# One more seven-product step in every first down pair of an MLP, with its rounding placed a group earlier

## The chip, the cores and the metric

The kernel runs on one core of one Trainium2 chip. The metric is the time of one execution in microseconds (us). Each kernel is measured in several runs, and the median counts. The traces come from one profiled execution per kernel.

## What is computed

The reference is one decoder block on 256 tokens with 2048 channels: attention and a state-space branch, merged by gates, and then an MLP. The change lies in the MLP alone:

```python
h = h + (g_attn * y_attn + g_ssm * y_ssm) @ w_out[layer]
u = rms_norm(h, mlp_norm_w[layer]) @ w_up[layer]          # 2048 -> 8192
h = h + jnp.square(jax.nn.relu(u)) @ w_down[layer]        # 8192 -> 2048
```

All is float32. The kernel splits each operand into a rounded high part and a remainder (`hi`, `lo`, both fp32r) and makes every product of three matmuls: hi by hi, lo by hi, hi by lo.

## The kernel before

**Pairs and groups.** The MLP is worked off in 16 *pairs* `m` (two column blocks of 512 each), in four rounds `q = m // 4` of one quarter of the 8192 channels. In a round `m % 4` is 0 or 1 for the two up pairs and 2 or 3 for the two down pairs. Each pair has 8 *groups* `j`. A group takes one 128 x 2048 load of weights (`raw4`, three buffers), which ScalarE rounds into `whi4` and VectorE turns into the remainder `wlo4` (two buffers each). A group (m, j) is written (2,5) below, where the first number is `m % 4`.

**Classical and seven.** A classical group makes 8 products of 128x128 by 128x512, that is 24 matmuls. A *seven* makes the same result by the Strassen-Winograd scheme with 7 products, 21 matmuls (`seven_products`, from L1134 on). It needs more from the other engines. VectorE makes sums of the weight tiles (`t_sums`, L2434 to L2439), ScalarE rounds them (`t_round`, L1723 and L1725), and VectorE makes the remainders `t_lo_` (L2424), which take the place of `t_sum`. For down pairs, four sums of activation tiles are made in each case (`f_sums`, L2505 to L2510), rounded (`f_sums_hi`, L1785), and their remainders made (`f_sums_lo`, L2514). A pair with sevens has four more PSUM banks, which are added up after the last seven of the pair (`p1_copy`, L1733, and `u_sums`, L2444 to L2449), and into `h` by `h_from_sums`. `seven(m)` gives the groups that are sevens. In the first down pair that is group 0 alone, in the second down pair 0, 3 and 5. Three forms of activation sums per round (for 0, 3, 5) are made anyway, since the second down pair uses them all.

**The order of work.** Every engine has its work in an order written out by hand, by (m % 4, j). At step j the engines prepare group j + 1: `mlp_hi` rounds its weights (L1712, or L1716 and L1718 for a seven), `mlp_lo` makes remainders (L2413, or L2418 for a seven). A seven with no seven in the two groups before it is `early`: its sums are made two groups ahead and rounded behind the weights of the group before it. `mlp_hi` waits until TensorE has let go of the buffer (`unit_used`), which for a seven means the whole group two before it.

**From an up pair to its down pairs.** At steps 0 to 5 of the next pair ScalarE works off the result of the up pair before: `relu` (L1740), `square` (L1755), `r_halve` (L1765, which splits float32 into halves of 16 bits for the transposing DMA), and, when SyncE's `r_turn` (L564) has brought the transposed halves, `f_hi` (L1777, L1781: joins the halves into `f_st`, then rounds them into `fT_hi`). VectorE follows with `f_lo` (L2521, `fT_lo`) and `f_sums`. `f_st` is one buffer: the second `f_hi` waits until `f_sums` has read the first. At (2,3) `f_hi` and `f_lo` stand before the weights of the next group (`JOIN_FIRST`), else behind them.

**Waits of TensorE.** At the head of a seven in a down pair TensorE waits for `sums_lo` of its form and for `fT_lo`. The first product of a pair that goes to banks 0 and 1 waits for `c_free`, which VectorE counts up when `h_from_banks` (L2467) has added the pair before into `h`. In a pair with a seven at group 0 that product is the one that begins with the 13th matmul.

**SyncE's queue.** It issues the loads of group j and, behind the loads of group 4 and of group 5, two transposes each (`TURN_AT`). It waits in order: for `lo_ready` of the group three before a load, and for `r_halve` before an `r_turn`.

Of the kernel before, what the change touches and what calls it, by code (L numbers as in the profile page):

```python
# [65 lines left out]
DOWN_SEVEN = (0, 3, 5)  # L66
DOWN_SEVEN_FIRST = (0,)
UP_ORDER = (0, 1, 2, 3, 4, 5, 6, 7)
# [31 lines left out]
H_SUMS = 1 if UP_SEVEN else 0  # L100
SUMS_AT = (6, 5, 5, 6)
SUMS_LATE = ((1, 6), (2, 3))
JOIN_FIRST = (2, 3)
MADE_FIRST = ()
FORMS_MADE = ((1, 4), (2, 1), (2, 3))
FORMS_HI = ((1, 5), (2, 4), (2, 5))
FORMS_LO = ((1, 6), (2, 5), (2, 6))
JOIN_AT = {1: (3, 5), 2: (3, 4)}
# [19 lines left out]
def build(nc, x, mix_norm_w, w_in, q_norm_w, k_norm_w, conv_w, conv_b, dt_bias, a_log, d_skip, ssm_norm_w,  # L128
# [13 lines left out]
    with ctx:  # L142
# [336 lines left out]
        def fp(ap):  # L479

            return ap.bitcast(f32)
# [35 lines left out]
        def _(sp):  # L517
# [213 lines left out]

            TURN_AT = (4, 5)
            for m in range(PAIRS):
# [485 lines left out]
        def _(act):  # L1219
# [577 lines left out]
            for m in range(PAIRS):  # L1797
# [3 lines left out]
                for j in range(QUADS):  # L1801
# [7 lines left out]
                    elif (m or j) and nxt[0] < PAIRS:  # L1809
                        if before is not None and (m % 4, j) == JOIN_FIRST:  # L1810
                            f_hi(before, JOIN_AT[m % 4].index(j))
                        mlp_hi(*nxt)
                        roundings(*nxt)
                    if before is not None:
# [4 lines left out]
                        if j == 1:  # L1819
                            r_halve(before, 0)  # L1820
                            square(before, 1)
# [4 lines left out]
                    for i, at_ in enumerate(FORMS_HI):  # L1826
                        if (m % 4, j) == at_:
                            f_sums_hi(m // 4, i)
# [11 lines left out]
        def _(dve):  # L1840
# [558 lines left out]

            def mlp_lo(m, j, only=None):  # L2400
                seven_, what = quads(m)[j]
# [14 lines left out]
                for i, part in enumerate((slice(1, 3), slice(3, 4))):  # L2416
                    dve.wait_ge(hi_ready, n + i + 1)
                    V.tensor_tensor(lo[:, part, :], src[:, part, :], fp(hi[:, part, :]), ALU.subtract).then_inc(lo_ready, 1)  # L2418
                for i in range(2):
                    part = slice(2 * i, 2 * i + 2)  # L2420
# [133 lines left out]
            for m in range(PAIRS):  # L2554
                k = m % 4
# [3 lines left out]
                for j in range(QUADS):  # L2559
# [6 lines left out]
                    elif j and nxt[0] < PAIRS:  # L2566
# [4 lines left out]
                        if is_seven(*nxt) and not early(*nxt):  # L2571
                            t_sums(*nxt)
                        mlp_lo(*nxt)
                    if early(*follow(m, j, 2)) and (k, j) in SUMS_LATE:
# [5 lines left out]
                    for i, at_ in enumerate(FORMS_LO):  # L2580
                        if (k, j) == at_:
                            f_sums_lo(m // 4, i)
# [187 lines left out]
```

## Time and profile before

| | us |
|---|---|
| median of 3 runs (lowest, highest) | 1977.62 (1977.33, 1977.79) |
| the profiled execution | 1977.46 |
| its span | 1975.4 |
| TensorE busy | 1968.7 |
| VectorE busy | 1488.0 |
| ScalarE busy | 1241.9 |

The span runs from the first to the last instruction; the execution's own time holds 2.1 us more. The profile's page gives the busy time of each engine. A matmul is shown with 0.39 us, but matmuls overlap, so what one costs is read from the distance of their starts. The same holds for VectorE and ScalarE, where an instruction may start about 0.1 us before the one before it ends. The timeline gives start, duration, engine, line and operands, with the idle time ahead in square brackets.

### The profile page before, as it was taken

To read this page: it belongs to the slowest core of one execution; us is meant where nothing else is said; L and a number is where in the kernel's file an instruction comes from. 1 tells how busy PE (TensorE), PEld (TensorE's weight loads), DVE (VectorE), ACT (ScalarE), POOL (GpSimd) and SP (SyncE) were. 2 spreads that over 40 slices of the span, in tenths; PEclk is the share of its full clock that TensorE was granted. 3 is DMA by queue.
4 is the path that set the end of the run, shared out by engine and by line. 5 is a ranking of instruction groups with operands and counts; after the bars stand their busy time and mean duration, and the time that the engine had idled before them with its cause. 6 is when DMAs were issued, how large, how long until landed. Compare 5 with 4: busy or idle time off the path is not lost.

```text
span 1975.4 us, 25599 instructions
## 1 busy us (share of the span) xinstructions
PE 1968.7 (100%) x9007; PEld 1629.1 (82%) x9007; DVE 1488.0 (75%) x1769; ACT 1241.9 (63%) x1427; POOL 175.1 (9%) x179
## 2 busy tenths in 40 slices
PE   9999999999999999999999999999999999999999
PEld 8888888888887888888888888888888888888887
DVE  5777777767788767676665556577898799888878
ACT  6666666767776555655674444557757855865773
POOL 2110020112232111111000000000000000000000
PEclk9999999999999999999999999999999999999999
DMA  7787887789987666665895776777666866676765
GB/s 250 207 205 201 213 205 210 213 222 247 235 228 229 197 194 200 199 194 182 218 246 190 213 214 229 213 213 217 221 201 202 245 196 208 215 224 202 229 198 171
DMA packets 332193, 419.52 MB, mean 212 GB/s; under 512 B 147248, under 2 KB 147696, under 8 KB 331840
## 3 DMA queue, kind: packets, MB, share of 16 engines
q1 hardware_dynamic: 331184, 415.23, 72.4%
q10 hardware_dynamic: 448, 2.24, 0.3%
q8 instruction: 59, 0.97, 0.2%
q0 software_dynamic: 464, 0.77, 0.2%
q14 instruction: 38, 0.31, 0.1%
HBM read 382.46 MB, written 2.16 MB: 195 GB/s over the span
## 4 chain that ended last, share of the span: by engine, by line
PE 98%; DVE 1%; ACT 1%; issue 0%; DVEq 0%; ACTq 0%
PE ps L807 20%; PE ps L809 20%; PE ps L808 20%; PE ps L1104 11%; PE ps L1109 11%; PE ps L1105 11%; PE ps L986 1%; PE ps L755 1%; PE ps L973 0%; DVE wlo L2413 0%; PE ps L819 0%; PE ps L858 0%; PE ps L881 0%; PE ps L1007 0%; ACT whi L1229 0%
## 5 line engine op out<-in xcount | busy, mean ns | idle before, releaser
L1848 DVE TENSOR_TENSOR wlo<-raw,whi 128x1024 fp32r<-128x1024 f32 x450 | 569.4, 1272 | 328.5 <-ACT whi L1229 327.0
L1229 ACT ACTIVATE whi<-raw 128x1024 fp32r<-128x1024 f32 x450 | 473.2, 1057 | 323.3 <-PE ps L809 313.1
L807 PE MATMUL ps<-whi,xT_hi 128*128 128x512 f32 x1268 | 498.3, 393 | 0.0
L809 PE MATMUL ps<-whi,xT_lo 128*128 128x512 f32 x1268 | 493.8, 389 | 0.0
L808 PE MATMUL ps<-wlo,xT_hi 128*128 128x512 f32 x1268 | 493.5, 389 | 0.0
L809 PEld LDWEIGHTS ps<-whi,xT_lo 128*128 128x128 f32 x1268 | 238.0, 188 | 50.2
L807 PEld LDWEIGHTS ps<-whi,xT_hi 128*128 128x128 f32 x1268 | 238.1, 188 | 48.9 <-issue 1.4
L808 PEld LDWEIGHTS ps<-wlo,xT_hi 128*128 128x128 f32 x1268 | 238.2, 188 | 47.3
L1712 ACT ACTIVATE whi<-raw 128x1024 fp32r<-128x1024 f32 x187 | 192.8, 1054 | 102.5 <-PE ps L1109 98.3
L2413 DVE TENSOR_TENSOR wlo<-raw,whi 128x1024 fp32r<-128x1024 f32 x186 | 219.7, 1220 | 41.4 <-ACT whi L1712 41.1
L1104 PE MATMUL ps<-whi,fT_hi 128*128 128x512 f32 x416 | 162.0, 389 | 0.2 <-DVE h L2467 0.2
L1105 PE MATMUL ps<-whi,fT_lo 128*128 128x512 f32 x416 | 161.8, 389 | 0.0
L1104 PE MATMUL ps<-whi,hT_hi 128*128 128x512 f32 x410 | 159.6, 389 | 0.0
L1105 PE MATMUL ps<-whi,hT_lo 128*128 128x512 f32 x410 | 159.5, 389 | 0.0
L1109 PE MATMUL ps<-wlo,fT_hi 128*128 128x512 f32 x416 | 114.0, 389 | 0.0
L1109 PE MATMUL ps<-wlo,hT_hi 128*128 128x512 f32 x410 | 112.1, 389 | 0.0
L807 PE MATMUL ps<-whi,sT_hi 128*128 128x512 f32 x256 | 99.6, 389 | 0.0
L808 PE MATMUL ps<-wlo,sT_hi 128*128 128x512 f32 x256 | 99.6, 389 | 0.0
L809 PE MATMUL ps<-whi,sT_lo 128*128 128x512 f32 x256 | 99.6, 389 | 0.0
L1104 PEld LDWEIGHTS ps<-whi,fT_hi 128*128 128x128 f32 x416 | 78.1, 188 | 17.0 <-ACT whi L1712 0.6
L1109 PEld LDWEIGHTS ps<-wlo,fT_hi 128*128 128x128 f32 x416 | 78.1, 188 | 16.2
L1105 PEld LDWEIGHTS ps<-whi,fT_lo 128*128 128x128 f32 x416 | 78.1, 188 | 16.2
(358 smaller groups left out, 2874.3 us busy)
## 6 DMA issues: line engine op xcount, KB each, us to landing
raw<-in_w_in SPq DMA_DIRECT2D x319, 512.0 KB, 4.3
raw<-in_w_up SPq DMA_DIRECT2D x128, 512.0 KB, 4.3
raw<-in_w_down SPq DMA_DIRECT2D x128, 512.0 KB, 4.7
raw<-in_w_ssm_out SPq DMA_DIRECT2D x64, 512.0 KB, 4.2
raw<-in_w_attn_out SPq DMA_DIRECT2D x32, 512.0 KB, 3.7
raw<-in_w_out SPq DMA_DIRECT2D x32, 512.0 KB, 4.3
arow<-arows SPq DMA_DIRECT2D x16, 512.0 KB, 4.9
x_in<-in_x SPq DMA_DIRECT2D x4, 512.0 KB, 7.8
```

The lines of the kernel that those rows point to most:

```text
L755: return nc.tensor.transpose(dst, src, ident[:, :])
L807: mm(dst, xh, whi[sl][:, kk, :], start=(s == 0 and kk == 0), stop=False)
L808: mm(dst, xh, wlo[sl][:, kk, :], start=False, stop=False)
L809: last = mm(dst, xl, whi[sl][:, kk, :], start=False, stop=(s == US - 1 and kk == UK - 1))
L986: last = mm(ps[6][d0:d0 + SHD, hh // 2 * P:(hh // 2 + 1) * P], xf[:, hh, :], M[:, hh, :], start=True, stop=True)
L1104: mm(ps[bank], xh, wh, start=first, stop=False)
L1105: mm(ps[bank], xl, wh, start=False, stop=False)
L1109: return mm(ps[bank], xh, wl, start=False, stop=(left[bank] == 0))
L1229: A(whi[s % SLOTS][:, :, :], raw[s % SLOTS][:, :, :], ACT.Copy).then_inc(hi_ready, 1)
L1712: A(dst[:, 2 * i:2 * i + 2, :], src[:, 2 * i:2 * i + 2, :], ACT.Copy).then_inc(hi_ready, 1)
L1848: V.tensor_tensor(wlo[s % SLOTS][:, :, :], raw[s % SLOTS][:, :, :], fp(whi[s % SLOTS][:, :, :]), ALU.subtract).then_inc(lo_ready, 1)
L2413: V.tensor_tensor(lo[:, part, :], src[:, part, :], fp(hi[:, part, :]), ALU.subtract).then_inc(lo_ready, 1)
```

## The change

`DOWN_SEVEN_FIRST` gets group 5 beside group 0, so that the four first down pairs (m = 2, 6, 10, 14) have two sevens in place of one. 33 sevens become 37. With it:

- ScalarE rounds the own weights of (2,5) and its sums behind the weights of (2,4), at step 3, and then the activation form for group 5 (`ROUND_LATE`). The second `f_hi` follows behind these.
- The activation forms of group 3 and 5 are rounded at (2,2) and (2,3), before at (2,4) and (2,5). Their remainders are made at (2,2) and, between the two parts of the own weights of (2,5), at (2,4).
- `r_halve` of the first block goes ahead of the weights of group 2, in every second up pair and every first down pair. Its transposes go behind the loads of group 3 and not of group 4 (`TURN_AT`).
- The sums of the banks of the first down pair move from step 5 to step 6 (`SUMS_AT`).

```diff
--- before.py
+++ after.py
@@ -64,7 +64,7 @@
 UP_SEVEN = (0, 3, 5)
 UP_SEVEN_LATE = (0, 3)
 DOWN_SEVEN = (0, 3, 5)
-DOWN_SEVEN_FIRST = (0,)
+DOWN_SEVEN_FIRST = (0, 5)
 UP_ORDER = (0, 1, 2, 3, 4, 5, 6, 7)
 UP_ORDER_LATE = (0, 1, 2, 3, 4, 5, 6, 7)
 DOWN_ORDER = (0, 1, 2, 3, 4, 5, 6, 7)
@@ -98,13 +98,14 @@
 
 
 H_SUMS = 1 if UP_SEVEN else 0
-SUMS_AT = (6, 5, 5, 6)
+SUMS_AT = (6, 5, 6, 6)
 SUMS_LATE = ((1, 6), (2, 3))
+ROUND_LATE = (2, 3)
 JOIN_FIRST = (2, 3)
 MADE_FIRST = ()
 FORMS_MADE = ((1, 4), (2, 1), (2, 3))
-FORMS_HI = ((1, 5), (2, 4), (2, 5))
-FORMS_LO = ((1, 6), (2, 5), (2, 6))
+FORMS_HI = ((1, 5), (2, 2), (2, 4))
+FORMS_LO = ((1, 6), (2, 2), (2, 4))
 JOIN_AT = {1: (3, 5), 2: (3, 4)}
 LOW_AT = {1: (4, 6), 2: (3, 4)}
 
@@ -729,7 +730,7 @@
                         for a in range(2):
                             r_turn(2 * p + TURN_AT.index(j), a)
 
-            TURN_AT = (4, 5)
+            TURN_AT = (3, 5)
             for m in range(PAIRS):
                 mlp_loads(m)
 
@@ -1809,22 +1810,29 @@
                     elif (m or j) and nxt[0] < PAIRS:
                         if before is not None and (m % 4, j) == JOIN_FIRST:
                             f_hi(before, JOIN_AT[m % 4].index(j))
-                        mlp_hi(*nxt)
-                        roundings(*nxt)
+                        if before is not None and j == 1:
+                            r_halve(before, 0)
+                        if (m % 4, j - 1) != ROUND_LATE:
+                            mlp_hi(*nxt)
+                        if (m % 4, j) == ROUND_LATE:
+                            mlp_hi(*follow(m, j, 2))
+                            t_round(*follow(m, j, 2))
+                            f_sums_hi(m // 4, FORMS_HI.index((m % 4, j + 1)))
+                        else:
+                            roundings(*nxt)
                     if before is not None:
                         if j == 0:
                             if before:
                                 relu(before)
                             square(before, 0)
                         if j == 1:
-                            r_halve(before, 0)
                             square(before, 1)
                         if j == 2:
                             r_halve(before, 1)
                         if j in JOIN_AT[m % 4] and (m % 4, j) != JOIN_FIRST:
                             f_hi(before, JOIN_AT[m % 4].index(j))
                     for i, at_ in enumerate(FORMS_HI):
-                        if (m % 4, j) == at_:
+                        if (m % 4, j) == at_ and (m % 4, j - 1) != ROUND_LATE:
                             f_sums_hi(m // 4, i)
                     if m == 0 and j == 1:
                         h_hi()
@@ -2397,7 +2405,7 @@
                 V.tensor_scalar(hs2[:, :], hs2[:, :], 1.0 / D, EPS, ALU.mult, ALU.add).then_inc(hmean_step, 1)
 
 
-            def mlp_lo(m, j, only=None):
+            def mlp_lo(m, j, only=None, between=None):
                 seven_, what = quads(m)[j]
                 n = M0 + 2 * (QUADS * m + j)
                 src, hi, lo = raw4[(QUADS * m + j) % 3], whi4[n // 2 % 2], wlo4[n // 2 % 2]
@@ -2416,6 +2424,8 @@
                 for i, part in enumerate((slice(1, 3), slice(3, 4))):
                     dve.wait_ge(hi_ready, n + i + 1)
                     V.tensor_tensor(lo[:, part, :], src[:, part, :], fp(hi[:, part, :]), ALU.subtract).then_inc(lo_ready, 1)
+                    if i == 0 and between is not None:
+                        f_sums_lo(*between)
                 for i in range(2):
                     part = slice(2 * i, 2 * i + 2)
                     dve.wait_ge(t_hi, 2 * v + i + 1)
@@ -2570,7 +2580,10 @@
                             f_sums(m // 4, FORMS_MADE.index((k, j)))
                         if is_seven(*nxt) and not early(*nxt):
                             t_sums(*nxt)
-                        mlp_lo(*nxt)
+                        if (k, j - 1) == ROUND_LATE:
+                            mlp_lo(*nxt, between=(m // 4, FORMS_LO.index((k, j))))
+                        else:
+                            mlp_lo(*nxt)
                     if early(*follow(m, j, 2)) and (k, j) in SUMS_LATE:
                         t_sums(*follow(m, j, 2))
                     if m and k in LOW_AT and j in LOW_AT[k] and (k, j) != JOIN_FIRST:
@@ -2578,7 +2591,7 @@
                     if (k, j) in FORMS_MADE and (k, j) not in MADE_FIRST:
                         f_sums(m // 4, FORMS_MADE.index((k, j)))
                     for i, at_ in enumerate(FORMS_LO):
-                        if (k, j) == at_:
+                        if (k, j) == at_ and (k, j - 1) != ROUND_LATE:
                             f_sums_lo(m // 4, i)
                     if m and j == 1 and (m - 1) % 4 >= 2 and seven(m - 1):
                         h_from_sums(m - 1)
```

## Rows read from the trace of the kernel before

**Rows 1.** The page: busy time of the engines, and the chain that ended last.

```profile
PE 1968.7 (100%) x9007; PEld 1629.1 (82%) x9007; DVE 1488.0 (75%) x1769; ACT 1241.9 (63%) x1427; POOL 175.1 (9%) x179
PE 98%; DVE 1%; ACT 1%; issue 0%; DVEq 0%; ACTq 0%
```

**Rows 2.** TensorE's waits from 1290 us on: total us, times, longest us.

```profile
PE ps L1104 <- DVE h L2467: 0.2, 1, 0.2
```

**Rows 3.** Timeline of TensorE: start, us, engine, line; pairs' first matmuls and two 13th ones.

```profile
1382.17 0.39 PE L1104 MATMUL ps<-whi,fT_hi 128*128 128x512 f32 x1
...
1425.01 0.39 PE L1104 MATMUL ps<-whi,fT_hi 128*128 128x512 f32 x1
...
1550.13 0.39 PE L1104 MATMUL ps<-whi,fT_hi 128*128 128x512 f32 x1
...
1595.85 0.39 PE L1104 MATMUL ps<-whi,fT_hi 128*128 128x512 f32 x1
...
1886.21 0.39 PE L1104 MATMUL ps<-whi,fT_hi 128*128 128x512 f32 x1
...
1932.20 0.47 PE L1104 MATMUL ps<-whi,fT_hi 128*128 128x512 f32 x1 [0.24 <-DVE h L2467]
```

**Rows 4.** Timeline of ScalarE, pair m = 2; the last row is from m = 14.

```profile
1386.85 1.06 ACT L1755 ACTIVATE ust<-ust 128x1024 f32<-128x1024 f32 x1
...
1389.71 1.90 ACT L1765 ACTIVATE r_half<-ust 128x2048 uint16<-128x2048 uint16 x1
...
1396.15 2.57 ACT L1777 ACTIVATE f_st<-f_half 128x1024 uint16<-128x1024 uint16 x2
1398.75 1.06 ACT L1781 ACTIVATE fT_hi<-f_st 128x1024 fp32r<-128x1024 f32 x1
1399.72 2.94 ACT L1712 ACTIVATE whi<-raw 128x1024 fp32r<-128x1024 f32 x3
...
1408.04 0.61 ACT L1785 ACTIVATE fs_hi<-fs_sum 128x512 fp32r<-128x512 f32 x1
...
1901.99 2.58 ACT L1777 ACTIVATE f_st<-f_half 128x1024 uint16<-128x1024 uint16 x2 [1.70 <-DMA f_half<-r_half]
```

**Rows 5.** Timeline of VectorE, pair m = 2; the last row is the end of m = 14.

```profile
1399.85 1.23 DVE L2521 TENSOR_TENSOR fT_lo<-f_st,fT_hi 128x1024 fp32r<-128x1024 f32 x1 [3.95 <-ACT fT_hi L1781]
1400.99 2.35 DVE L2413 TENSOR_TENSOR wlo<-raw,whi 128x1024 fp32r<-128x1024 f32 x2
1403.26 0.28 DVE L2505 TENSOR_TENSOR fs_sum<-f_st 128x128 f32<-128x128 f32 x1
...
1404.19 2.35 DVE L2413 TENSOR_TENSOR wlo<-raw,whi 128x1024 fp32r<-128x1024 f32 x2
...
1412.40 0.69 DVE L2514 TENSOR_TENSOR fs_lo<-fs_sum,fs_hi 128x512 fp32r<-128x512 f32 x1
1413.00 0.69 DVE L2444 TENSOR_TENSOR ust<-ps,ust 128x512 f32<-128x512 f32 x1
...
1415.59 1.22 DVE L2434 TENSOR_TENSOR t_sum<-raw 128x1024 f32<-128x1024 f32 x1
...
1418.18 2.35 DVE L2413 TENSOR_TENSOR wlo<-raw,whi 128x1024 fp32r<-128x1024 f32 x2
...
1421.05 1.82 DVE L2418 TENSOR_TENSOR wlo<-raw,whi 128x1024 fp32r<-128x1024 f32 x2
1422.79 2.35 DVE L2424 TENSOR_TENSOR t_lo__92<-t_sum,t_hi__93 128x1024 fp32r<-128x1024 f32 x2
...
1930.83 2.35 DVE L2467 TENSOR_TENSOR h<-ps,h 128x1024 f32<-128x1024 f32 x2
```

**Rows 6.** SyncE's first transposes of m = 2; median us from issue to landing.

```profile
1391.63 2.61 SPq L564 DMA_TRANSPOSE f_half<-r_half  x2
...
raw<-in_w_down SPq DMA_DIRECT2D x32, 512.0 KB, 4.7
f_half<-r_half SPq DMA_TRANSPOSE x8, 3.6
```

## The prediction, made before the changed kernel was run

> **What bounds the kernel now.** I read the page first: TensorE is busy for 1968.7 of 1975.4 us, and 98% of the chain that ended last is its own work [rows 1]. Its list of waits came next. In the whole MLP the wait on `h` appears once, with 0.2 us [rows 2]. So time can come only from fewer matmuls, and any wait that the change brings is paid in full. Third, the timeline of TensorE gives the price of a matmul. The pair m = 2 has one seven and seven classical groups, 21 + 7 x 24 = 189 matmuls, and runs from 1382.17 to 1425.01, 42.84 us [rows 3]. That is 0.2267 us for each (the 0.39 us shown is a duration with overlap). A classical group is 5.44 us, a seven 4.76. Last I read ScalarE and VectorE around steps 1 to 7 of a first down pair, in their order, since there the new work goes. The reader is to see that VectorE idles for 3.95 us and then starts on `fT_lo` only when ScalarE delivers `fT_hi` [rows 5]. Idle time ahead of that start is of no use to the new work, which all comes behind it.
>
> **What is saved.** Four groups lose 3 matmuls each: 12 x 0.2267 = 2.72 us, or 0.68 in each of the pairs 2, 6, 10, 14. This is all the gain there can be, apart from one stall of the present kernel, below. The Trainium skill (TensorE: Matmul & The Clock Gate, "Step-by-step: what each phase is for") gives 216 ns for a 512-column matmul back to back. By it the saving would be 2.59 us; the trace has the longer distance, and it is used.
>
> **ScalarE up to the first join.** All times are for m = 2. `square` starts at 1386.85 and takes 1.06 [rows 4]. `r_halve` now follows at once and reads what `square` wrote. Where a step reads the one before, it starts 0.03 behind its end (1396.15 + 2.57, then 1398.75 [rows 4]), not 0.10 ahead of it. So `r_halve` starts at 1387.94 and ends at 1389.84, 1.8 us sooner than now (1389.71 + 1.90 [rows 4]). The weights of group 2 go 1.9 us later and are ready at 1390.8; TensorE wants them at 1381.94 + 4.76 + 5.44 = 1392.1 (a pair's weight load starts 0.23 before its first matmul), so this move is covered, and costs up to its size only if the cover of 1.3 us were gone. The remainder, 2.3 us for two, is asked for 8 matmuls later and is covered too. Up to the join the same pieces run as before, plus the 0.13 us of the dependence and the rounding of the form for group 3, 0.52 us (0.61 [rows 4] less the overlap). The join moves from 1396.15 to 1396.80, `fT_hi` to 1399.40. VectorE starts `fT_lo` 1.10 behind that start (1398.75, 1399.85 [rows 4, 5]): 1400.50.
>
> **The transposes.** SyncE now waits for `r_halve` ahead of group 4's loads, until 1389.9, and spends 2.61 us on two transposes [rows 6]. Group 4's loads go at about 1392.5, and by the median of 4.7 us [rows 6] land at 1397.2 or a little later. ScalarE wants them at 1400.4. The transposes land at about 1392.5 + 3.6 = 1396.1, and the join is ready for them at 1396.8. In this pair they are worth nothing, since ScalarE is the later one today too (no idle time ahead of 1396.15 [rows 4]). In m = 14 the join waits 1.70 us for them today [rows 4], all behind it comes later, and TensorE waits for `h` [rows 2, 3]. There the earlier transposes take the join's wait away, and so this pair loses least in the sum below. In the second up pairs the same move only touches covered work.
>
> **VectorE from there on.** This is the term that decides. Start to start, all from [rows 5]: `f_lo` 1.14 (1399.85 to 1400.99); a pair of remainders, `wlo` or `t_lo`, 2.27 (1400.99 to 1403.26), one 1.14; `f_sums` 0.93; `f_sums_lo` 0.60; `u_sums` 2.59; `t_sums` 2.59 (1415.59 to 1418.18); own weights of a seven 1.74 (1421.05 to 1422.79), which is 1.14 + 0.60. In the new order:
>
> - from 1400.50: `f_lo` 1.14, `wlo` of (2,4) 2.27, `t_sums` of (2,5) 2.59, `f_sums` 0.93, first part of own weights 1.14, `f_sums_lo` 0.60: 1409.17, finished some 0.1 later, at 1409.3.
> - then second part 0.60, `t_lo` 2.27, `f_lo` 1.14, `wlo` of (2,6) 2.27, `t_sums` of (3,0) 2.59, `wlo` of (2,7) 2.27, `u_sums` 2.59, own weights of (3,0) 1.74, `t_lo` 2.27: 1426.91, where `h_from_banks` starts.
>
> ScalarE keeps ahead of this. It takes up (2,5)'s weights when TensorE lets go of group 3 (about 1403.5), and its second join can start at 1408.1, so `f_lo` (wanted at 1412.0) finds `fT_hi`. That is why "a group ahead" buys nothing for the weights of (2,5): the wait for group 3 holds them where they are now. What it buys is that `f_hi` no longer stands between them and the sums.
>
> **What TensorE sees.** First wait: it reaches (2,5) at 1381.94 + 4.76 + 4 x 5.44 = 1408.46 and waits for `sums_lo` until 1409.4, 0.9 us. Behind it on TensorE stand all 21 matmuls of the group, the own-weight products too, though their inputs are ready. Second wait: the 13th matmul of the next pair needs `c_free`. In m = 14 today `h` starts at 1930.83 [rows 5] and that matmul at 1932.20 [rows 3], 1.37 later. With `h` at 1426.91 it starts at 1428.28, which is 46.11 us behind the pair's first matmul. Because VectorE has no idle time between the two waits, the first one is contained in the second: only the 46.11 counts. Today's distance is 42.84 + 12 x 0.2267 = 45.56 for m = 2, and I take the same for m = 10. It is 1595.85 - 1550.13 = 45.72 for m = 6 and 1932.20 - 1886.21 = 45.99 for m = 14 [rows 3]. The net loss is 0.55 + 0.39 + 0.55 + 0.12 = 1.6 us. Against the profiled execution that is a span of 1977.0 and a time of 1979.1; its own time is 0.16 under the median, so against the median it is 1979.2. I forecast 1979.2.
>
> The step that is hardest to bound is the landing of the weights of (3,0). They are issued behind `wlo` of (2,5), at about 1410.4 for the second half, and wanted by `t_sums` at 1415.45. That leaves 5.1 us against a median of 4.7 [rows 6].
>
> A rule of the skill speaks against the change. VectorE: DVE Perf Modes, "The DRAIN you can't avoid", says that the next operation doesn't start until the pipe has emptied. If nothing overlapped, each of VectorE's steps would cost its full duration, and the path would be longer by its overlaps. The trace shows two remainders in 2.35 us and the next start 2.27 us after the first.
>
> **Rivals.** *Covered* (chance 0.12): VectorE and ScalarE keep up after all, and the whole saving stays: 1977.6 - 2.7 = 1974.9. The change would do in full what it says. For it: VectorE is busy for 75% only. Against it: the path above needs to be 1.2 us shorter in each pair, and its idle time lies before 1400. *No overlap* (0.03): each remainder costs VectorE its duration of 1.22 us [rows 5] instead of 1.14. There are 14 on the path, so it is 14 x 0.08 = 1.1 us more in each pair, 4.5 in all: 1983.7. *Late weights*, slower than before and beyond what can be measured as no change (0.13): the loads of (3,0) take 6.1 us instead of 4.7, because SyncE issues transposes and loads in a denser row. From 5.1 us on each microsecond is paid at the second wait, 4 in all: 1983.2. The same would be so for (2,5). *The second wait is absorbed* (0.17): `h` comes early enough, and the first wait alone stays: 0.9 - 0.68 = 0.2 in each pair, 1978.5. *The forecast* (0.55): 1979.2, by itself between 1977.8 and 1981.2, since 0.1 us on the path is 0.4 us in all.
>
> **How the numbers follow.** A measurement of this kernel can tell about 0.2%, or 4.0 us, from no change: 1973.7 and 1981.6 are the bounds. Nothing but an unforeseen gain is below the first, since the saving is 2.7 (0.02). Above the second are the late weights, the missing overlap and the tail of the forecast (0.16). The rest is 0.82. The range 1976.0 to 1983.0 leaves out the covered case and half of the cases above 1981.6.
>
> **What would show it.** Right: 12 matmuls fewer; in each first down pair a wait of TensorE on `fs_lo` of 0.7 to 1.2 us at group 5; one on `h` of 0.2 to 0.6 us at the next pair's 13th matmul; VectorE without idle time from `fT_lo` to `h`; the first matmuls of the pairs m = 3, 7, 11, 15 about 0.3 us later after their pair's start than now; no ScalarE wait for the first transposes. Wrong: idle time of VectorE in that stretch, released by a DMA or by ScalarE, or no wait of TensorE on `h`.

## The result and the profile after

| | before | after |
|---|---|---|
| median (lowest, highest) | 1977.43 (1976.82, 1978.06) of 22 runs | 1980.22 (1979.10, 1980.96) of 22 runs |
| the profiled execution and its span | 1977.46, 1975.4 | 1980.47, 1978.4 |
| TensorE busy | 1968.7 | 1968.2 |
| VectorE busy | 1488.0 | 1504.2 |
| ScalarE busy | 1241.9 | 1248.5 |

The ratio is 1.0014, 95% interval 1.0008 to 1.0020: the kernel with 12 matmuls fewer is 2.8 us slower. The forecast was 1979.2, 1.6 us slower. In the table of the next section two single slow executions are left out of the medians, 4215.86 us of `e3_gate_late` and 9164.91 us of `e11_sums_first`.

The page of the changed kernel, its busy times and the engines' shares of the chain that ended last, as in [rows 1]:

```profile
PE 1968.2 (99%) x8995; PEld 1626.1 (82%) x8995; DVE 1504.2 (76%) x1789; ACT 1248.5 (63%) x1435; POOL 175.1 (9%) x179
...
PE 85%; DVE 8%; ACT 4%; issue 2%; DMA 1%; SPq 0%; DVEq 0%; ACTq 0%
```

The matmuls fell from 9007 to 8995, as meant. But TensorE's share of the last chain went from 98% to 85%. VectorE and ScalarE now stand in it. The list of TensorE's waits in the MLP (sum, times, longest), first for matmuls, then for weight loads, answers to [rows 2]:

```profile
PE ps L1105 <- issue: 2.0, 4, 0.5
PE ps L1105 <- DVE h L2477: 1.7, 5, 0.6
...
PEld ps L1105 <- ACT whi L1713: 3.6, 5, 0.9
PEld ps L1105 <- issue: 3.6, 4, 0.9
```

There was one wait of 0.2 us on `h`, and there are five now. Four more stand at (2,5). They are shown as "issue", which means that the profile names no releaser; that it is the form's remainder `fs_lo` is read from the times below. The weight load of the same product shows 0.90 us of idle time, the matmul 0.50. Neither is what the wait costs. What counts is the distance of the matmuls' starts. TensorE in m = 2 and at the head of m = 3 (start, duration, engine, line, operands; idle time ahead in brackets), against [rows 3]:

```profile
1382.44 0.39 PE L1105 MATMUL ps<-whi,fT_hi 128*128 128x512 f32 x1
...
1409.60 0.19 PEld L1105 LDWEIGHTS ps<-whi,fT_hi 128*128 128x128 f32 x1 [0.90 <-issue]
1409.63 0.47 PE L1105 MATMUL ps<-whi,fT_hi 128*128 128x512 f32 x1 [0.50 <-issue]
1409.94 0.39 PE L1106 MATMUL ps<-whi,fT_lo 128*128 128x512 f32 x1
...
1428.83 0.47 PE L1105 MATMUL ps<-whi,fT_hi 128*128 128x512 f32 x1 [0.55 <-DVE h L2477]
1429.13 0.40 PE L1106 MATMUL ps<-whi,fT_lo 128*128 128x512 f32 x1
```

Without a wait the added seven would start 117 matmuls behind the pair's first, at 1382.44 + 117 x 0.2267 = 1408.96. It starts at 1409.63, 0.67 us late, and its second matmul comes 0.31 behind the first in place of 0.23. So the first wait is worth 0.75 us. From the pair's first matmul to the next pair's 13th it is 1428.83 - 1382.44 = 46.39 us. In the other three it is 46.11, 46.12 and 46.10, where 46.11 was forecast. VectorE, from the first `f_lo` to `h`, against [rows 5]:

```profile
1400.77 1.23 DVE L2531 TENSOR_TENSOR fT_lo<-f_st,fT_hi 128x1024 fp32r<-128x1024 f32 x1 [2.86 <-ACT fT_hi L1782]
1401.91 2.35 DVE L2421 TENSOR_TENSOR wlo<-raw,whi 128x1024 fp32r<-128x1024 f32 x2
1404.18 1.22 DVE L2444 TENSOR_TENSOR t_sum<-raw 128x1024 f32<-128x1024 f32 x1
...
1408.84 0.69 DVE L2524 TENSOR_TENSOR fs_lo<-fs_sum,fs_hi 128x512 fp32r<-128x512 f32 x1
...
1416.00 1.23 DVE L2444 TENSOR_TENSOR t_sum<-raw 128x1024 f32<-128x1024 f32 x1 [0.20 <-DMA raw<-in_w_down]
...
1427.46 2.35 DVE L2477 TENSOR_TENSOR h<-ps,h 128x1024 f32<-128x1024 f32 x2
```

From `fT_lo` at 1400.77 to `h` at 1427.46 VectorE idles once, for 0.20 us, at the sums of (3,0). In the other three rounds it doesn't idle there at all. `fs_lo` ends at 1409.53, and the seven starts at 1409.63.

### The profile page after: what moved, and what is told of

The parts are those of the page before. It is cut to its first block, busy times and chain, and to the rows that moved or that the text cites. A ratio compares the mean times of both kernels' runs of the same rounds, so it can differ in the third digit from the quotient of the medians.

```text
span 1978.4 us, 25603 instructions
## 1 busy us (share of the span) xinstructions
PE 1968.2 (99%) x8995; PEld 1626.1 (82%) x8995; DVE 1504.2 (76%) x1789; ACT 1248.5 (63%) x1435; POOL 175.1 (9%) x179
## 4 chain that ended last, share of the span: by engine, by line
PE 85%; DVE 8%; ACT 4%; issue 2%; DMA 1%; SPq 0%; DVEq 0%; ACTq 0%
PE ps L808 20%; PE ps L809 20%; PE ps L810 20%; PE ps L1105 7%; PE ps L1106 7%; PE ps L1110 7%; DVE wlo L2421 2%; DVE t_lo__92 L2434 1%; DVE wlo L2426 1%; ACT f_st L1778 1%; DVE t_sum L2444 1%; PE ps L987 1%; DMA raw<-in_w_down 1%; PE ps L756 1%; ACT whi L1713 1%
## 5 line engine op out<-in xcount | busy, mean ns | idle before, releaser
L1856 DVE TENSOR_TENSOR wlo<-raw,whi 128x1024 fp32r<-128x1024 f32 x450 | 569.3, 1272 | 327.6 <-ACT whi L1230 325.9
L1230 ACT ACTIVATE whi<-raw 128x1024 fp32r<-128x1024 f32 x450 | 473.1, 1057 | 321.8 <-PE ps L810 316.0
L1713 ACT ACTIVATE whi<-raw 128x1024 fp32r<-128x1024 f32 x179 | 184.5, 1054 | 101.9 <-PE ps L1110 101.6
L2421 DVE TENSOR_TENSOR wlo<-raw,whi 128x1024 fp32r<-128x1024 f32 x178 | 210.1, 1219 | 42.0 <-ACT whi L1713 41.8
L1105 PE MATMUL ps<-whi,fT_hi 128*128 128x512 f32 x392 | 153.2, 391 | 3.4 <-issue 2.0
L1106 PE MATMUL ps<-whi,fT_lo 128*128 128x512 f32 x392 | 152.5, 389 | 0.0
L1110 PE MATMUL ps<-wlo,fT_hi 128*128 128x512 f32 x392 | 107.9, 389 | 0.0
L1105 PEld LDWEIGHTS ps<-whi,fT_hi 128*128 128x128 f32 x392 | 73.6, 188 | 21.6 <-issue 3.6
L1105 PEld LDWEIGHTS ps<-whi,hT_hi 128*128 128x128 f32 x410 | 77.0, 188 | 16.6 <-ACT whi L1713 0.7
L1110 PEld LDWEIGHTS ps<-wlo,hT_hi 128*128 128x128 f32 x410 | 77.0, 188 | 16.0
```

The lines of the kernel that those rows point to most:

```text
L1105: mm(ps[bank], xh, wh, start=first, stop=False)
L1106: mm(ps[bank], xl, wh, start=False, stop=False)
L1110: return mm(ps[bank], xh, wl, start=False, stop=(left[bank] == 0))
L1230: A(whi[s % SLOTS][:, :, :], raw[s % SLOTS][:, :, :], ACT.Copy).then_inc(hi_ready, 1)
L1713: A(dst[:, 2 * i:2 * i + 2, :], src[:, 2 * i:2 * i + 2, :], ACT.Copy).then_inc(hi_ready, 1)
L1856: V.tensor_tensor(wlo[s % SLOTS][:, :, :], raw[s % SLOTS][:, :, :], fp(whi[s % SLOTS][:, :, :]), ALU.subtract).then_inc(lo_ready, 1)
```

## The experiments

Each of these twelve kernels is a variant of the changed one, except the first. Times are medians, and each ratio is to runs of the kernel before on the same chip. The span is that of the profiled execution. The distances from a first down pair's first matmul to the next pair's 13th, and from round to round, are read from the same traces. They are the better measure of what an edit did, because two things outside it vary from kernel to kernel: the start of the first down pair m = 2 (1381.76 to 1382.44 over all fourteen kernels), and a wait at the head of m = 12, which is shown further down.

| kernel | time | ratio to before (95%) | span |
|---|---|---|---|
| e1_moves_alone | 1976.81 | 0.9997 (0.9988 to 1.0005) | 1974.7 |
| e2_turns_back | 1979.84 | 1.0011 (1.0002 to 1.0020) | 1977.8 |
| e8_extra_behind | 1984.72 | 1.0037 (1.0023 to 1.0050) | 1982.6 |
| e5_second_f_lo_out | 1978.76 | 1.0008 (0.9999 to 1.0017) | 1976.7 |
| e4_first_f_lo_out | 1979.21 | 1.0010 (1.0001 to 1.0019) | 1977.2 |
| e3_gate_late | 1979.58 | 1.0010 (1.0001 to 1.0019) | 1977.6 |
| e9_form_on_pool | 1982.45 | 1.0025 (1.0015 to 1.0034) | 1981.0 |
| e10_sums_turns_back | 1977.32 | 1.0001 (0.9992 to 1.0010) | 1977.0 |
| e11_sums_first | 1990.54 | 1.0068 (1.0055 to 1.0081) | 1987.3 |
| e12_load5_first | 1983.21 | 1.0029 (1.0017 to 1.0041) | 1980.6 |
| e13_form3_later | 1985.53 | 1.0040 (1.0026 to 1.0054) | 1983.7 |
| e14_both_ends | 1976.42 | 0.9995 (0.9986 to 1.0004) | 1973.7 |

### The moves without the sevens

On the kernel before: `r_halve` of the first block ahead of the weights of group 2, its transposes behind the loads of group 3.

```diff
-            TURN_AT = (4, 5)
+            TURN_AT = (3, 5)
...
+                        if before is not None and j == 1:
+                            r_halve(before, 0)
                         mlp_hi(*nxt)
...
-                            r_halve(before, 0)
```

> The kernel before with only the two moves of the change: the first r_halve ahead of the weights of group 2, and the first block's transposes behind group 3's loads. No seven is added. Theory (VectorE's path from the first f_lo to h, lengthened by the seven, sets the loss): the moves cost nothing, and may give back up to 0.4 us, since in m = 14 the join no longer waits 1.7 us for the transposes and the wait on h at the pair's end goes. 1977.0 to 1977.5. Rival (the moves delay ScalarE's weights or SyncE's loads and are part of the loss): 1 to 2 us slower than before, with waits of TensorE on whi or of VectorE on raw in the pairs 1, 2, 5, 6, 9, 10, 13, 14.

Measured: 1976.81, 0.65 us under the kernel before in the medians, with an interval that holds 1. Not one wait of TensorE is left in the MLP. The moves cost nothing. What they give is about what the kernel before loses in m = 6 and m = 14, 0.16 and 0.43 us over 45.56 [rows 3]. So the loss comes from the sevens and the orders of work that go with them.

### The place of the transposes

The changed kernel with `TURN_AT` back at the loads of group 4.

```diff
-            TURN_AT = (3, 5)
+            TURN_AT = (4, 5)
```

> The changed kernel with the first block's transposes back behind group 4's loads; all else as changed. Theory: SyncE's loads of group 4 go out before r_halve is done, so the transposes are issued at the same time as in the changed kernel and only share the DMA engines with the loads. The join waits for them by 0 to 1 us, and each such microsecond lengthens the path in that pair: 1980.2 to 1982. Rival (the move to group 3 holds up loads, and that is in the loss): the time falls by 0.5 us or more, under 1979.7.

Measured: 1979.84, 0.4 us under the changed kernel and within the scatter of both. The same nine waits are there, and the distance to the 13th matmul is 46.11, 46.18, 46.12 and 46.12 us:

```profile
PE ps L1105 <- issue: 2.1, 4, 0.5
PE ps L1105 <- DVE h L2477: 1.5, 5, 0.3
```

ScalarE waits nowhere for the transposes. Their earlier place is worth nothing here, and the prediction's credit for m = 14 is owed to the earlier `r_halve`, if to a move at all.

### One more step on VectorE's path

One remainder of 1.14 us, of no use to the result, right behind the first `f_lo` of each first down pair (`V.tensor_tensor(fT_lo[:, 12:16, :], ...)`, whose result is overwritten later).

> The changed kernel with one more subtraction of 4 x 256 elements on VectorE (1.14 us; it writes a part of fT_lo that is written again before use) directly behind the first f_lo, in each of the four first down pairs. Theory (VectorE's work from the first f_lo on is a gapless path): both waits of TensorE are reached 1.1 us later, the one at (2,5) is 2.0 us, and the time is 4 x 1.14 = 4.6 us more: 1984.8. Rival (a part of the path is ScalarE's: with the first f_lo left out, VectorE waited 0.8 us for the weights of (2,4)): that part is no cover for added work, so the number is the same; but if VectorE had slack before the second wait, the time would be 1982 or less.

Measured: 1984.72, 4.5 us over the changed kernel, or 1.1 us in each of the four pairs for a step of 1.14 us. The wait at (2,5) grew by the same amount, the one on `h` did not grow:

```profile
PE ps L1105 <- issue: 6.6, 4, 1.7
PE ps L1105 <- DVE h L2477: 1.7, 5, 0.5
```

The distance to the 13th matmul is 47.24 us once and 47.25 three times, that is 46.11 + 1.14. As expected, the step is paid once and in full in each of the four pairs, and not once for each wait. That is the containment of the prediction, read in the other direction.

### One step less between the two waits

Of the second `f_lo`, all but one element is left out in m = 6, 10, 14, so the remainder of the second block of `fT` is not computed there.

```diff
+                n = (1, 1) if (m % 4, a) == (1, 1) and m > 4 else (4, T)
```

> The same amount of work left out in the same pairs, but of the second f_lo, which lies behind the first wait and ahead of the second. Theory: the first wait stays, 0.9 us. The one on h goes, but it was only 0.3 to 0.55 us over what the first leaves: 3 x 0.35 = 1.1 us less, 1979.1. Rival (same worth wherever it lies): 1977.1 as in the kernel above.

Measured: 1978.76. The wait at (2,5) stays. Of the three pairs with the cut, the one on `h` goes from the list behind m = 10 and m = 14 and stays behind m = 6. It also goes at m = 12:

```profile
PE ps L1105 <- issue: 2.0, 4, 0.5
PE ps L1105 <- DVE h L2477: 0.6, 2, 0.3
...
1581.03 2.36 DVE L2421 TENSOR_TENSOR wlo<-raw,whi 128x1024 fp32r<-128x1024 f32 x2 [0.54 <-ACT whi L1713]
```

The distances to the 13th matmul are 46.05, 45.86 and 45.75 us, so 0.06, 0.26 and 0.35 came back. VectorE lost nearly all of a step of 1.14 us, but then waited 0.54 us for ScalarE's weights of (2,6) (the last row, m = 6), and in m = 6 another 0.32 for the weights of (3,0). TensorE's own 198 matmuls up to there take 198 x 0.2267 = 44.89 us, so with the first wait alone the distance would be 44.89 + 0.75 = 45.64, which none of the three reaches. The rest of the 1.5 us under the changed kernel lies outside these pairs. The time came near the expected 1979.1, but not for the reason given there.

### One step less ahead of both waits

The same for the first `f_lo`, so the remainder of the first block of `fT` is not computed in m = 6, 10, 14.

```diff
+                n = (1, 1) if (m % 4, a) == (1, 0) and m > 4 else (4, T)
```

> The changed kernel; in the pairs 6, 10 and 14 the first f_lo subtracts one element in place of 4 x 256 (the remainder of that block of fT is left out there). VectorE's path becomes 1.0 us shorter at its head, ahead of both waits. Theory: the first wait of TensorE goes, at (2,5), and the one on h is 0 to 0.2 us: 3 x 1.0 = 3.1 us less, 1977.1. Rival (any microsecond taken off VectorE between 1400 and 1427 is worth the same, wherever it lies): the same time here as in the next kernel.

Measured: 1979.21, where 1977.1 was expected. The distances to the 13th matmul are 45.89, 45.89 and 45.88 us, so only 0.22 came back in each pair instead of the expected 1.0. VectorE in m = 6:

```profile
1568.70 0.16 DVE L2532 TENSOR_TENSOR fT_lo<-f_st,fT_hi 128x1 fp32r<-128x1 f32 x1 [2.86 <-ACT fT_hi L1782]
1569.65 2.36 DVE L2421 TENSOR_TENSOR wlo<-raw,whi 128x1024 fp32r<-128x1024 f32 x2 [0.79 <-ACT whi L1713]
```

The step still takes 0.16 us, and 0.79 us of waiting for ScalarE's weights of (2,4) follow, which come behind `fT_hi` there. From `f_lo` to the remainders it is 0.95 us (1569.65 - 1568.70), against 1.15 in the changed kernel. At its head the path belongs to both engines, and VectorE stands only 0.20 us (1.15 - 0.95) behind ScalarE. The prediction called it VectorE's path alone, and by it a faster VectorE is overrated.

These two kernels were meant to tell the theory from its rival, that a microsecond taken off VectorE is worth the same wherever it lies. They can't. In the three pairs together each cut gave 0.67 us, since ScalarE bounds VectorE behind both.

### The gate behind two products

TensorE's wait for `sums_lo` at (2,5) behind the first two products' high parts, which don't read the form. The own weights were ready.

```diff
-                    if not up:
+                    late = m % 4 == 2 and j == 5
+                    if not up and not late:
...
-                        own_high(p1, p2, p3)
+                        own_high(p1, p2)
+                        if late:
+                            pe.wait_ge(sums_lo, H_SUMS + len(DOWN_SEVEN) * (m // 4) + f + 1)
+                        own_high(p3)
```

> The changed kernel, but in the added seven (2,5) TensorE waits for the remainder of the activation form only ahead of its third product, behind four matmuls that don't need it. Theory (the first wait is contained in the second, since VectorE is busy without a gap between them): the wait of 0.9 us at (2,5) all but goes, the one on h at the next pair's 13th matmul grows by as much, to 1.2 to 1.5 us, and the time stays: 1979.9 to 1980.4. Rival (the waits add up): 4 x 0.9 = 3.6 us less, 1976.6.

Measured: 1979.58, 0.6 us under the changed kernel. The wait at the head of (2,5) is gone, and its time reappears at the head of the next pair, on `t_lo_` and `h`:

```profile
PE ps L1105 <- DVE h L2481: 2.9, 4, 0.7
...
PEld ps L1110 <- DVE t_lo__92 L2438: 2.5, 8, 0.4
...
1428.08 0.47 PE L1105 MATMUL ps<-whi,fT_hi 128*128 128x512 f32 x1 [0.72 <-DVE h L2481]
```

The distances to the 13th matmul are 46.11, 46.12, 46.12 and 46.13 us, as with the first wait. So in these pairs nothing was gained by taking it away. The 0.6 us lie outside them: the first down pair starts 0.47 us earlier (1381.97 against 1382.44), and VectorE's wait of 0.20 us in m = 2 isn't there. This shows that the first wait was contained in the second. A rival that gave the first wait a price of its own expected 3.6 us.

### The form on GpSimd

`f_sums` and `f_sums_lo` for group 5 go to the idle GpSimd, the rounding of the form ahead of the weights of (2,5).

```diff
+                            f_sums_hi(m // 4, FORMS_HI.index((m % 4, j + 1)))
                             mlp_hi(*follow(m, j, 2))
                             t_round(*follow(m, j, 2))
-                            f_sums_hi(m // 4, FORMS_HI.index((m % 4, j + 1)))
...
+                G.tensor_tensor(fs_lo[:, i, :, :], fs_sum[:, i, :, :], fp(fs_hi[:, i, :, :]), ALU.subtract) \
+                    .then_inc(sums_lo, 1)
```

> The changed kernel with the activation form of group 5 made on the idle GpSimd (four sums of 128x128 and their remainder of 128x512), and its rounding on ScalarE ahead of the weights of (2,5). This takes 0.93 + 0.60 = 1.5 us off VectorE's path in each first down pair, and the form is there long before group 5. Theory: the path needs to be 1.2 us shorter, so both waits go and the whole 2.7 us are gained, with 0.4 more in m = 14: 1974.3 to 1975.3, faster than both kernels. Rival (GpSimd disturbs VectorE or is too slow): VectorE's operations grow longer or TensorE waits on GpSimd at (2,5), 1977 or more.

Measured: 1982.45, slower still. VectorE and GpSimd at the join of m = 2:

```profile
1400.65 1.33 DVE L2531 TENSOR_TENSOR fT_lo<-f_st,fT_hi 128x1024 fp32r<-128x1024 f32 x1 [2.87 <-ACT fT_hi L1782]
1401.91 3.72 DVE L2421 TENSOR_TENSOR wlo<-raw,whi 128x1024 fp32r<-128x1024 f32 x2
...
1400.45 0.46 POOL L2769 TENSOR_TENSOR fs_sum<-fs_sum,f_st 128x128 f32<-128x128 f32 x1
1400.98 1.33 POOL L2771 TENSOR_TENSOR fs_sum<-f_st,fs_sum 128x128 f32<-128x128 f32 x1
1403.12 1.43 POOL L2774 TENSOR_TENSOR fs_lo<-fs_sum,fs_hi 128x512 fp32r<-128x512 f32 x1 [0.81 <-ACT fs_hi L1786]
...
1412.92 1.23 DVE L2531 TENSOR_TENSOR fT_lo<-f_st,fT_hi 128x1024 fp32r<-128x1024 f32 x1 [0.69 <-ACT fT_hi L1782]
```

Two remainders take 3.72 us beside GpSimd's last two steps, and 2.35 us without them (1401.91 of the changed kernel, above). A GpSimd step of a size that takes 0.46 us alone takes 1.33 us where it meets `fT_lo`. Of the 1.53 us that left VectorE (0.93 + 0.60), 1.37 (3.72 - 2.35) came back as blocking. The Trainium skill (SBUF — State Buffer, "SBUF: two separate sides") says that the two share a port pair as an exclusive lock, held for a whole instruction. The rows agree: both engines' steps are longer where they meet.

So VectorE won next to nothing, and there is a second effect. Its weight sums come 1.37 us later, ScalarE rounds them later, and with that the second join is late: VectorE waits 0.69 us for `fT_hi` (last row), where the changed kernel has no wait. The distance to the 13th matmul is 46.83 to 46.85 us in place of 46.11. In the medians the kernel is 2.2 us slower than the changed one.

### The weight sums ahead of the first f_lo, in four orders

VectorE idles for 2.86 us ahead of the first `f_lo`, and the sums of (2,5) cost 2.59. They need only the raw weights. Four kernels put them there. First with the transposes behind the loads of group 4:

```diff
-SUMS_LATE = ((1, 6), (2, 3))
+SUMS_LATE = ((1, 6),)
...
-            TURN_AT = (3, 5)
+            TURN_AT = (4, 5)
```

> The changed kernel with the weight sums of (2,5) (t_sums, 2.59 us) made ahead of the first f_lo and not behind the remainders of (2,4), where VectorE stands idle for 2.9 us until fT_hi is there; and the first transposes back behind group 4's loads, so that group 5's weights are loaded ahead of that time (issued at about 1393.5, landed at 1398.2). Theory (what lies behind fT_lo on VectorE decides): the path becomes 2.6 us shorter where 1.2 are needed; both waits go: 1974.2 to 1975.3, faster than both kernels. Rival (the weights land late, VectorE is held by them and f_lo comes later): TensorE waits for fT_lo at group 4, 1976 or more.

Measured: 1977.32 (its profiled execution took 1979.03). The weights of group 5 were issued at once and landed late:

```profile
1389.86 2.84 SPq L565 DMA_TRANSPOSE f_half<-r_half  x2
1393.21 0.37 SPq L714 DMA_DIRECT2D raw<-in_w_down  x1
1393.63 0.46 SPq L715 DMA_DIRECT2D raw<-in_w_down  x1
...
1400.85 1.23 DVE L2444 TENSOR_TENSOR t_sum<-raw 128x1024 f32<-128x1024 f32 x1 [3.23 <-DMA raw<-in_w_down]
```

From the second issue to the landing it is 1400.85 - 1393.63 = 7.2 us in m = 2 and 6.3, 5.8 and 6.0 us in m = 6, 10 and 14, against a median of 4.6 for all such loads of this kernel. `fT_lo` started at 1403.45 in place of 1400.77, and TensorE waited for it.

Then with `TURN_AT = (3, 5)`, as in the changed kernel:

> As the kernel above, but with the transposes where the change has them, behind group 3's loads. Group 5's weights are then issued only at 1395.0 and 1395.5 and land at about 1400. Theory: VectorE waits for them until about 1400.1 and makes f_lo at 1402.7 in place of 1400.8; TensorE wants fT_lo at group 4 (1403.3) and gets it at about 1403.9, 0.5 us late in each of four pairs: 1976 to 1977. Rival (the order in SyncE's queue doesn't matter): the same as the kernel above.

Measured: 1990.54, the slowest, where 1976 to 1977 was expected. The loads of group 4 now stand between the transposes and group 5:

```profile
1401.76 1.23 DVE L2444 TENSOR_TENSOR t_sum<-raw 128x1024 f32<-128x1024 f32 x1 [4.10 <-DMA raw<-in_w_down]
...
DVE t_sum L2444 <- DMA raw<-in_w_down: 17.8, 5, 5.0
...
PE ps L1105 <- DVE fT_lo L2531: 10.0, 4, 3.1
```

The second of these is the sum of VectorE's waits for these loads, the third what TensorE waited for `fT_lo`. A step in VectorE's idle time that waits on a DMA can hold everything behind it, and here it did.

Third, all loads of group 5 ahead of the transposes, `TURN_AT = (5, 6)`, with `r_halve` back behind the weights of group 2:

> The added seven with the sums of group 5 ahead of the first f_lo, as in e10. There the weights of group 5 were issued at 1393.6 and landed only at 1400.8, behind and beside four transposes. Here r_halve is back behind the weights of group 2, as in the kernel before, so that the remainders of (2,2) are made 1.9 us sooner, and the two pairs of transposes go behind the loads of group 5 and 6. Group 5's weights are then issued at 1391.3, ahead of all transposes. Theory: they land by 1397.5, the sums are made in VectorE's idle time until 1400.4, f_lo starts at 1401.0 to 1402, both waits go, and TensorE waits at most 0.4 us for fT_lo where the transposes are late (m = 14): 1974.5 to 1975.8, faster than both kernels. Rival (the transposes, now behind the loads, hold the join by over 1.5 us): TensorE waits for fT_lo at group 4 in each pair, 1977 or more.

Measured: 1983.21. The sums run in the idle time, in m = 2 at 1397.62 without a wait, in m = 6 and 10 behind waits of 0.54 and 0.98 us. Now the transposes are late, and ScalarE's join waits:

```profile
1397.62 1.22 DVE L2443 TENSOR_TENSOR t_sum<-raw 128x1024 f32<-128x1024 f32 x1
...
1399.06 2.58 ACT L1778 ACTIVATE f_st<-f_half 128x1024 uint16<-128x1024 uint16 x2 [2.08 <-DMA f_half<-r_half]
```

The median of the transposes' landing went from 3.5 us in the changed kernel to 4.9. Fourth, the same with the form of group 3 rounded behind the join instead of ahead of it, to bring the join forward:

> As e12, and the activation form of group 3 is rounded on ScalarE behind the join and the weights of (2,4), in the time in which ScalarE waits for TensorE, and its remainder made on VectorE behind the sums of group 5's form. The join on ScalarE can come 0.5 us sooner, if the transposes are there. Theory: where e12 still has a wait for fT_lo it becomes smaller, 0 to 0.5 us less per pair, 1974.3 to 1975.5. Rival (the join waits for the transposes, not for ScalarE): the same as e12 within 0.3 us.

Measured: 1985.53. TensorE's waits for `fT_lo` rose (5.3 us in place of 4.2), those on `h` went from three to five, and those at (2,5) came back. The join was bound by the transposes, so nothing came forward, and ScalarE had one step more behind it.

A gain over the changed kernel came of one of the four, 2.9 us, and less than was expected; the other three lost. The term that failed each time was the landing time: medians were taken for loads and transposes that stand beside each other. Why these land late was not tested.

### The form ahead of the first f_lo, and h in two steps

The last kernel uses the idle time for a step that waits on no DMA beyond the join itself: `f_sums` for the form of (2,5) runs behind `f_st`, while ScalarE still makes `fT_hi`, and ScalarE rounds that form ahead of the weights of (2,5). It also splits the first half of `h`'s update, so that bank 0 is free one step of 512 columns sooner.

```diff
-                    if bank in (0, 1, 6, 7) and first and m:
+                    if bank == 0 and first and m and (m - 1) % 4 >= 2:
+                        pe.wait_ge(bank0_free, sum(1 for i in range(m) if i % 4 >= 2))
+                    elif bank in (0, 1, 6, 7) and first and m:
...
+                for a in range(2):
+                    part = h_pair(m, 0)[:, a * COLS:(a + 1) * COLS]
+                    V.tensor_tensor(part, ps[a], part, ALU.add).then_inc((bank0_free, c_free)[a], 1)
...
+                        if (k, j) == ROUND_LATE:
+                            f_sums(m // 4, FORMS_MADE.index((k, j)))
```

> The changed kernel with two edits. (a) In pairs 2, 6, 10 and 14 the sum for the forms of group 4 on VectorE (f_sums, 0.93 us start to start) goes ahead of the first f_lo, where VectorE waits 2.86 us for ScalarE's f_hi anyway, and ScalarE rounds those forms ahead of the weights of group 5. (b) In all pairs the first half of h's update is done in two steps of 512 columns with a semaphore of its own behind the first, so that the next pair's 13th matmul waits for the first step alone, some 0.53 us sooner. Nothing of the computation is left out. My theory (VectorE's gapless path behind the first f_lo sets both waits): the path is 0.93 us shorter, so the wait of 0.91 us at (2,5) shrinks to at most 0.1; from the pair's first matmul to the next pair's 13th the chain is 46.11 - 0.93 - 0.53 = 44.65 us, less than TensorE's own 44.88, so the wait on h goes too; span 1972.5 to 1974.5, time 1974.3 to 1976.0, some 4 to 6 us under the changed kernel and 1.5 to 3 under the kernel before. Rival (ScalarE's weights are as late as VectorE's path, as where the first f_lo was cut to one element and only 0.25 to 0.35 us came of it): the wait at (2,5) keeps 0.5 to 0.7 us, and the time is 1976 to 1978, no better than before.

The form meant there is the one of the seven at (2,5). Measured: 1976.42, 3.8 us under the changed kernel. It is 0.9 us under the kernel before on the same chip, with an interval that holds 1, so a gain over that kernel isn't shown. It is 0.4 us above the expected range; the span, 1973.7 in the profiled execution and 1974.4 in the median one, lies in its own. VectorE at the join, and at the head of m = 3 with TensorE:

```profile
1399.46 0.29 DVE L2519 TENSOR_TENSOR fs_sum<-f_st 128x128 f32<-128x128 f32 x1 [1.77 <-ACT f_st L1781]
...
1400.56 1.23 DVE L2535 TENSOR_TENSOR fT_lo<-f_st,fT_hi 128x1024 fp32r<-128x1024 f32 x1
...
1426.20 1.28 DVE L2481 TENSOR_TENSOR h<-ps,h 128x512 f32<-128x512 f32 x2
1427.39 1.21 DVE L2482 TENSOR_TENSOR h<-ps,h 128x1024 f32<-128x1024 f32 x1
...
1427.34 0.40 PE L1109 MATMUL ps<-whi,fT_lo 128*128 128x512 f32 x1
1427.62 0.47 PE L1108 MATMUL ps<-whi,fs_hi 128*128 128x512 f32 x1
...
1428.39 0.40 PE L1113 MATMUL ps<-wlo,fs_hi 128*128 128x512 f32 x1
1428.75 0.47 PE L1108 MATMUL ps<-t_hi__93,fT_hi 128*128 128x512 f32 x1
```

The wait at (2,5) is gone in all four pairs. The edit to `f_sums` did this, since the one to `h` comes behind it; what each gave at the 13th matmul was not measured alone. The step that left the path stood behind the weights of (2,4), where ScalarE had bounded the earlier cut, and so the rival didn't come true. The 13th matmul starts at 1427.11, with no idle time ahead, 44.89 us behind the pair's first at 1382.22, which is TensorE's own pace. What is left of the wait on `h` are small gaps at the next products. Each follows a step of VectorE: the second `h` step ends at 1427.48, a matmul starts at 1427.62; the third ends at 1428.60, the next product starts at 1428.75. The starts there are 0.28, 0.31, 0.36 and 0.31 us apart in place of 0.23, some 0.35 us in all.

The distance from the first matmul of a first down pair to the first of the next round's up pair shows the whole bill. For m = 6 and 7 it is 1634.61 - 1550.13 = 84.48 us before, 1636.31 - 1551.35 = 84.96 after, and 1633.91 - 1549.90 = 84.01 here. Two pairs without any wait take 84.32 (m = 2 and 3 before: 1466.49 - 1382.17), and with three matmuls fewer 83.64. So of the 0.68 us in a round, 0.31 (84.32 - 84.01) is kept. Four times that is 1.2 us, and the span is 1.0 us under that of the moves alone. In the medians it is only 0.4 us (1976.81 - 1976.42), because the profiled execution of the last kernel ran 0.7 us under its own median. That is within the scatter of both.

## Why the prediction was right

- **The saving.** 12 matmuls of 0.2267 us, 2.7 us, is what the trace has: where no wait stands, the pairs run at that distance.
- **The first wait.** Forecast 0.9 us at (2,5), on the form's remainder. It is 0.90 to 0.91 at the weight load in m = 2, 6, 10 and 14. The moment was forecast as 1409.4 and is 1409.6, with the whole pair 0.27 us later. But a weight load that had to wait starts 0.03 us ahead of its matmul (1409.60, 1409.63) and otherwise 0.23. In the matmuls' starts the wait is 0.75 us, and so the first matmuls of m = 3, 7, 11 and 15 stand 42.94 to 42.96 us behind their pair's start, 0.1 more than the undisturbed 42.84 and not the forecast 0.3. The sum didn't use this. The rival *the second wait is absorbed*, which put 0.2 us a pair on the first wait alone, overrated it.
- **The second wait and containment.** Forecast 46.11 us to the next pair's 13th matmul, measured 46.39, 46.11, 46.12 and 46.10. The extra step (47.25, one step of 1.14 more) and the late gate (46.11 to 46.13 without the first wait) bear it out. The cuts of the two `f_lo` don't: ScalarE bounded both.
- **The size.** Forecast +1.6 us, measured +2.8 in the medians and +3.0 in the spans. Four terms were missing, 1.4 us in all. The MLP's first down pair starts 0.27 us later (1382.44 against 1382.17), which is no part of the change: over all the kernels run here that start varies from 1381.76 to 1382.44. In m = 2 the raw weights of (3,0) came 5.4 us behind their issue (1410.57 to 1416.00), and VectorE waited 0.20. The step called the hardest to bound, with its limit of 5.1 us, was the right one to name. The idle time of VectorE that came of it, released by a DMA, is one of the two signs that the prediction gave for being wrong. It came in one round of four, and it cost 0.28 us (46.39 - 46.11) where the rival *late weights* had 4. A matmul that follows a wait is followed by the next 0.31 us later in place of 0.23, and that 0.08 us was counted nowhere. It is paid at the waits on `h`, which were one and are now five, so 0.3 us more; the 0.08 at (2,5) is contained in the second wait like the first wait itself. And from m = 12 to m = 14 it is 84.16 us in place of 83.64 (1889.06 - 1804.90, before 1886.21 - 1802.57), half a microsecond more, with a new wait at the head of m = 12:

```profile
1795.23 1.23 DVE L2444 TENSOR_TENSOR t_sum<-raw 128x1024 f32<-128x1024 f32 x1 [2.14 <-DMA raw<-in_w_up]
...
1808.05 0.47 PE L1105 MATMUL ps<-whi,hT_hi 128*128 128x512 f32 x1 [0.26 <-DVE h L2477]
```

  The weights for m = 12 were issued at 1788.98 and landed at 1795.23, 6.3 us later, and VectorE got to `h` late. The kernel before and the moves alone have no such wait. Every kernel here with the added sevens has this wait of VectorE once, at the same place, at 1.5 to 2.7 us. So late weights did cost time, but it was another load than the one that the prediction bounded. Why it comes in one round only, and why the sevens bring it, is open.
- **ScalarE keeps ahead.** Right for the second join, but too weak for the first stretch: with the first `f_lo` cut, VectorE ran into ScalarE after 0.20 us. The forecast didn't rest on it, the remedy would have.
- **The transposes.** The forecast gave them no worth in m = 2 and some in m = 14. Put back, they cost nothing anywhere.
- **The rivals.** *Covered* fell: both waits are there in all four rounds, and VectorE's path is as long as was summed. *No overlap* fell: 1400.77 to 1401.91 and 1401.91 to 1404.18 are 1.14 and 2.27 us, as before. *The second wait is absorbed* fell: it stands in all four rounds.

## What to carry to other kernels

On an engine without idle time, follow its steps from the last point where it waited to the point where the bounding engine waits for it. Of several waits behind one such path only the latest counts, and taking away an earlier one gains nothing (46.12 us with and without the first wait). Before you shorten such a path, look how far behind it the next engine is: here it was 0.20 us. To shorten the path, move into the idle time ahead of it a step whose inputs are there already, not one that waits for a DMA. Freeing a shared resource in the smallest piece that its first reader needs went with it here; its own share wasn't measured.

## What was not expected of the hardware

- Loads issued right behind two transposes landed late: 512 KB after 7.2, 6.3, 5.8 and 6.0 us in the four rounds, where the kernel's median was 4.6. With the transposes behind the loads of group 5 their median was 4.9 us, against 3.5.
- VectorE's two remainders took 3.72 us instead of 2.35 beside two GpSimd steps, and a GpSimd step of a size that otherwise took 0.46 us took 1.33.
- After a wait of TensorE the second matmul starts 0.30 or 0.31 us behind the first, not 0.23. It is so at all nine waits of the changed kernel, and at those with 1.65 us of idle time of the kernel with the extra step. After waits for `fT_lo` it was 0.33 or 0.34.
